# Rank-dependent slot sizes in a two-layer mixture of experts, and a tile's norm placed inside the sum of rows

## The chip, the cores and the metric

One core of a Trainium2 chip runs the whole program in one launch. The metric is the device time of one execution in microseconds. The changed kernel runs on the same core with the same inputs.

## The reference, cut to what matters

Two layers over 256 latent tokens and 256 context tokens of width 1024, all in float32. Each layer mixes tokens with four head groups, and then runs a mixture of experts with 64 routed experts, 6 per token, and one shared expert. Layer 0 routes 512 tokens (3072 assignments, 48 per expert on average), layer 1 only the 256 latent tokens (1536 assignments, 24 on average).

```python
scores = sigmoid(h @ router_w);  idx = top_k(scores + router_bias, 6)
gates = 2.5 * scores[idx] / sum(scores[idx])
y = sum over the 6 experts e of  gate * ((silu(h @ w_gate[e]) * (h @ w_up[e])) @ w_down[e])
y = y + shared expert(h);        x = x + mod[5] * y
# the next layer begins with   h = rms_norm(x) * (gain * (1 + mod[1])) + mod[0],   p = h @ w_in
```

An expert has 1024 x 768 gate and up weights and 384 x 1024 down weights: 4.72 MB, 302 MB for the 64 experts of a layer.

With the inputs that the reference draws by default, the experts sorted by how many tokens chose them have these counts. Layer 0: fullest 112, then 103, fifth 81, sixteenth 65, seventeenth 64, the twelve emptiest 24 down to 11. Layer 1: fullest 61, fifth 48, seventeenth 32, the twelve emptiest 8 down to 3.

## The kernel before, in words

**Units.** The experts are ranked by their count on the chip. A unit is one pass of 128 token slots through TensorE. The WHOLE fullest experts have a unit of 128 slots each (16 in layer 0, 4 in layer 1). The others go in pairs, 64 slots each, so that UNITS is 40 in layer 0 and 34 in layer 1. In a paired unit each contraction step is two matmuls, one on array columns 0 to 63 with one expert's weights streaming and one on columns 64 to 127 with the other's. The trace calls these 128*64, and those of a whole unit 128*128; each float32 matmul of these lines leaves two records. Assignments that don't fit their expert's slots go to an overflow list; if there are any, a loop over all 64 experts for each tile of tokens runs afterwards (more_slots). It did not run in this profile.

**Weights.** An expert's weights come as three chunks of 1.5 MB (lo, hi, down), each loaded by SP into one of 8 buffers, in the order in which the units use them (load_chunk, L847). SP waits for each load until the chunk that last held the buffer has been used: lo and hi are freed by the matmuls of L1425, down by those of L1446. `work(l)` writes the order of the units: 2 whole ones, then the pairs with the other whole ones spread among them, no whole one late. Units of the shared expert have their weights loaded once; layer 0 has four of them, two before the routed ones and two after the first and second routed one.

**A unit on the engines.** POOL gathers its 128 rows (L2475), PE transposes them (L1406), DVE copies them (L2302, L2303), PE runs gate and up (unit_up: lo, then hi, L1425), ACT and DVE make the activation (L1728, L2166), PE transposes it (L1437) and ACT copies it (L1734), PE runs down (L1446), ACT and DVE copy it out (L1747, L2321), and POOL scatters the rows to y_d (L2481). DVE makes the ranks, capacities and slot addresses while PE runs the shared expert (L2215 to L2248), PE turns them into lists (L1343).

**The sum of rows (`combined`).** After the last unit, SP loads for each tile of 128 tokens the six rows of each token (yrow, three buffers, L887), and after the third of these loads the next layer's first two modulation rows (load_mod, L757). PE sums five of the six rows with diagonal matrices (L948), DVE adds the sixth (L1837), adds PE's sum, multiplies and adds to xs (L1843 to L1845), ACT squares (L1523), DVE and ACT make the standard deviation (L1853, L1525), DVE makes h (`finished`, L1830 to L1832), PE transposes h (L962), ACT copies it. PE's order is: tile 0, tile 1, transposes of tile 0, tile 2, transposes of tile 1, tile 3, transposes of tiles 2 and 3. `finished(i - 1)` stands on DVE behind the adds of tile i, and DVE waits for the modulation rows (`mod_loaded`) behind the adds of tile 0. SP then waits until PE has summed tile 2, issues the next layer's projection weights (load_projection, L762 to L765) and its 16 small loads (load_small, L769 to L772), and all engines meet at the end of the phase. The first projection matmuls follow (L976). The row of L913 below is from the start of the program, where the modulation is computed with matmuls on four 32-column tiles.

## Time and profile before

| | |
|---|---|
| runs before | 2777.4, 2782.1, 2788.86 us; median 2782.1 |
| profiled execution | 2787.68 us, its span 2785.5 us |
| TensorE busy | 2377.6 us, 85% of the span |
| VectorE, ScalarE, GpSimd busy | 27%, 16%, 12% |
| mean granted TensorE clock | 0.941 of 2.4 GHz |
| DMA | 776.12 MB, mean 279 GB/s |
| routed units of layer 0 | from about 624 to 1467 us of the span |
| sum of rows, layer 0 to layer 1 | 1484.6 to 1564.7 us |
| routed units of layer 1 | from about 1970 to 2736 us |

Times of rows are microseconds from the start of the span. A busy TensorE is not one at its peak: its matmuls overlap, and while it waits for weights nothing is counted. What bounds a stage is read from which wait ends last there, and from the DMA share and rate of that stretch.

### The profile page before, as it was taken

The numbers are of one execution on the slowest core, as the hardware profiler recorded it, in microseconds if no ns is written. First come the engines' busy times: TensorE is split into PE (matmuls) and PEld (weight loads), VectorE is DVE, ScalarE is ACT, GpSimd is POOL, SyncE is SP. The second block draws the span as 40 slices with busy tenths as digits, with TensorE's granted clock in tenths as the row PEclk, the third lists the DMA queues.
The fourth block names the chain that finished last, engine by engine and source line by source line (L and its number), as shares of the span: only waits on it lengthen the run. The fifth ranks groups of instructions, "written<-read, shape, count | busy, mean of one in ns | idle before, by whom it ended". The sixth has DMA issues, their size and how long they took to land. (4 is left out here: it accounts for less than half of the span.)

```text
span 2785.5 us, 38829 instructions
## 1 busy us (share of the span) xinstructions
PE 2377.6 (85%) x16229; PEld 1276.6 (46%) x16229; DVE 742.8 (27%) x1589; ACT 443.1 (16%) x901; POOL 323.0 (12%) x380
## 2 busy tenths in 40 slices
PE   4998999989989998889884898998888788788885
PEld 2457744455444444444431356854443334343332
DVE  1364545353111111111102446464210101111111
ACT  1232343210000000000000132352000000000000
POOL 0005300000111111110100003400111111000000
PEclk8999999999999999999997899999999999999997
DMA  8000088445999999999985310015699999999993
GB/s 304 25 21 32 4 317 312 170 153 179 413 427 415 405 409 393 396 399 380 418 345 215 118 46 17 4 66 207 251 425 427 421 422 421 414 413 411 411 413 127
DMA packets 126595, 776.12 MB, mean 279 GB/s; under 512 B 36760, under 2 KB 45096, under 8 KB 69968
## 3 DMA queue, kind: packets, MB, share of 16 engines
q1 hardware_dynamic: 103376, 735.75, 65.4%
q0 software_dynamic: 23040, 37.82, 3.7%
q8 instruction: 133, 2.18, 0.3%
q14 instruction: 46, 0.38, 0.0%
HBM read 770.98 MB, written 44.44 MB: 293 GB/s over the span
## 5 line engine op out<-in xcount | busy, mean ns | idle before, releaser
L1425 PE MATMUL banks<-arena,htreg 128*64 128x384 f32 (+1 forms) x4288 | 922.4, 522 | 184.7 <-DMA arena<-in_exp_w_gu 177.6
L1425 PEld LDWEIGHTS banks<-arena,htreg 128*64 128x64 f32 (+1 forms) x4288 | 455.0, 156 | 622.8 <-issue 388.8
L1446 PE MATMUL banks<-arena,modreg 128*64 128x512 f32 (+1 forms) x1608 | 433.4, 599 | 23.9 <-issue 19.7
L2166 DVE TENSOR_TENSOR modreg<-modreg,banks 128x384 f32<-128x384 f32 x80 | 44.3, 554 | 1063.1 <-ACT modreg L1728 1059.4
L1446 PEld LDWEIGHTS banks<-arena,modreg 128*64 128x64 f32 (+1 forms) x1608 | 155.4, 148 | 245.5 <-issue 242.0
L2475 POOL DMA_INDIRECT htreg<-h_d,lsg x74 | 76.2, 1029 | 1059.6 <-PE banks L1406 929.7
L988 PE MATMUL banks<-arena,htreg 128*128 128x512 f32 (+3 forms) x480 | 159.7, 492 | 0.0
L2321 DVE COPY modreg<-banks 128x512 f32<-128x512 f32 x74 | 51.2, 692 | 319.7 <-PE banks L1446 319.7
L2481 POOL DMA_INDIRECT y_d<-modreg,lst x74 | 73.4, 992 | 478.3 <-DVE modreg L2321 477.7
L1728 ACT ACTIVATE modreg<-banks 128x384 f32<-128x384 f32 x80 | 39.2, 490 | 562.9 <-PE banks L1425 562.9
L1734 ACT ACTIVATE modreg<-banks 128x384 f32<-128x384 f32 x80 | 39.2, 490 | 517.9 <-PE banks L1437 517.9
L988 PEld LDWEIGHTS banks<-arena,htreg 128*128 128x128 f32 x480 | 89.9, 191 | 65.5 <-issue 61.5
L1747 ACT ACTIVATE modreg<-banks 128x512 f32<-128x512 f32 x74 | 44.2, 597 | 448.5 <-PE banks L1446 448.5
L948 PE MATMUL banks<-arena 128*128 128x512 f32 x120 | 60.5, 668 | 56.1 <-DMA arena<-y_d 56.1
L976 PE MATMUL banks<-htreg,arena 128*128 128x512 f32 x192 | 85.7, 609 | 14.4 <-SPq L667 13.7
L1406 PEld LDWEIGHTS banks<-const,htreg 128*128 128x128 f32 x592 | 73.8, 193 | 46.6 <-issue 31.6
L1406 PE MATMUL banks<-const,htreg 128*128 128x128 f32 x592 | 84.2, 286 | 9.1 <-DMA htreg<-h_d,lsg 9.1
L1290 PE MATMUL banks<-arena,htreg 128*128 128x512 f32 x192 | 83.2, 593 | 0.0
L1245 PE MATMUL banks<-arena 64*128 64x512 f32 (+3 forms) x144 | 73.0, 589 | 2.6 <-ACT arena L1662 2.6
L948 PEld LDWEIGHTS banks<-arena 128*128 128x128 f32 x120 | 25.8, 219 | 89.6 <-issue 89.6
L976 PEld LDWEIGHTS banks<-htreg,arena 128*128 128x128 f32 x192 | 37.5, 196 | 61.7 <-issue 46.6
L1080 PE MATMUL banks<-arena 64*64 64x64 f32 x1536 | 59.2, 224 | 0.9 <-issue 0.6
(393 smaller groups left out, 2183.9 us busy)
## 6 DMA issues: line engine op xcount, KB each, us to landing
arena<-in_exp_w_gu SPq DMA_DIRECT2D x256, 1536.0 KB, 23.9
arena<-in_exp_w_down SPq DMA_DIRECT2D x128, 1536.0 KB, 23.4
arena<-in_w_mod SPq DMA_DIRECT2D x32, 1024.0 KB, 10.2
arena<-y_d SPq DMA_DIRECT2D x6, 3072.0 KB, 16.8
modreg<-in_w_mod SPq DMA_DIRECT2D x14, 1024.0 KB, 8.5
modreg<-mod_d SPq DMA_DIRECT2D x20, 512.0 KB
arena<-in_w_in SPq DMA_DIRECT2D x4, 2048.0 KB, 9.4
arena<-in_w_out SPq DMA_DIRECT2D x2, 4096.0 KB, 14.1
```

Of the source, the lines that this page charges most:

```text
L948: last = mm(ps[4 + 2 * (i % 2) + half][:], diag[i % 2][:, k, :], yrow[i % YB][:, k, 512 * half:512 * half + 512], start=(k == 0), stop=(k ...
L976: last = mm(ps[ct % 2][:], win_qkv[:, k, tok(ct)], hT[:, k, :], start=(k == 0), stop=(k == KD - 1))
L988: last = mm(ps[2 + n % 4][:, lo:w], hT[:, k, tok(t)], win[g][:, k, lo:w], start=(k == 0), stop=(k == KD - 1))
L1080: last = mm(out[r, at + HALF * g:at + HALF * g + HALF], lhs(r, g), rhs(r, g), start=True, stop=True)
L1245: mm(ps[s % 2][:, 0:nk * P], q_, k_, start=True, stop=True).then_inc(scores_psum.sem, 1)
L1290: last = mm(ps[2 + n % 2][:], mixT[:, k, tok(t)], wout[:, k, 512 * half:512 * half + 512], start=(k == 0), stop=(k == KD - 1))
L1406: last = pe.transpose(ps[k // 4][:, tok(k % 4)], src[:, k, :], ident)
L1425: last = mm(gu_bank(n, half)[rows, 0:DE], src[:, k, rows], up4[q][:, i, DE * half:DE * (half + 1)], start=(k == 0), stop=(k == KD - 1))
L1446: last = mm(ps[4 + half][rows, :], actT[:, k, rows], dn3[q][:, k, 512 * half:512 * half + 512], start=(k == 0), stop=(k == KE - 1))
L2321: dve.tensor_copy(outs[r % 2][:, 512:1024], ps[5][:]).then_inc(unit_y.sem, 1)
L2475: pool.indirect_dma_start(out=slots[r % 2], out_offset=None, in_=h_d, in_offset=bass.IndirectOffsetOnAxis(ap=lsg1[:, u:u + 1], axis=0), bo ...
L2481: pool.indirect_dma_start(out=y_d, out_offset=bass.IndirectOffsetOnAxis(ap=lst1[:, u:u + 1], axis=0), in_=outs[r % 2], in_offset=None, bou ...
```

## The change

Layer 0 has 4 whole units instead of 16. In both layers the fifth to sixteenth fullest experts (BIG = 12) have 96 slots and share a unit with one of the twelve emptiest, which has 32. The others stay in pairs of 64. Layer 0 then has 34 units instead of 40, layer 1 has 34 as before. A unit of 96 and 32 slots is run as four 32-column tiles per contraction step, three with the one expert's weights and one with the other's (tiles_of). DVE's ranks, capacities and addresses follow the three sizes. In the sum of rows, DVE waits for the modulation rows and finishes tile i - 1 before its adds of tile i; SP issues the modulation rows after the second load of rows, and the small loads ahead of its wait and of the projection weights.

```diff
--- before.py
+++ after.py
@@ -38,7 +38,8 @@
 NT = 4
 MIX = 1024
 HALF = P // 2
-WHOLE = (16, 4)
+WHOLE = (4, 4)
+BIG = (12, 12)
 UNITS = tuple((NE + w) // 2 for w in WHOLE)
 CHUNK = 3072
 SLOTS = 8
@@ -339,7 +340,7 @@
         unit_hot = carve(stat, 288, NE)
         row64 = carve(stat, 352, NE)
         shift_by = carve(stat, 416, NE)
-        keycol, rankcol, dropcol = (carve(stat, 480 + i, 1) for i in range(3))
+        keycol, rankcol, dropcol, latecol = (carve(stat, 480 + i, 1) for i in range(4))
         maxcnt = sb("maxcnt", [1, 8], I32)
         RING = 4
         eid = sb("eid", [P, NE], U32)
@@ -571,7 +572,9 @@
         def work(l):
 
             whole = [(u, (u,)) for u in range(WHOLE[l])]
-            paired = [(u, (u, u + UNITS[l] - WHOLE[l])) for u in range(WHOLE[l], UNITS[l])]
+            big = range(WHOLE[l], WHOLE[l] + BIG[l])
+            paired = [(u, (u, u + NE - big.stop)) for u in big]
+            paired += [(u, (u, u + UNITS[l] - big.stop)) for u in range(big.stop, UNITS[l])]
             order = [whole.pop(0) for _ in range(FIRST)]
             early = len(paired) - 4
             for i in range(len(paired)):
@@ -886,13 +889,13 @@
                         sp.wait_ge(out_psum.sem, out_psum.at(2 * l + 1, 2 * (i - YB) + 2))
                     sp.dma_start(yrow[i % YB], y_d.rearrange("(t p k) d -> t p k d", p=P, k=CODES)[i, :, 0:TOPK, :]
                                  ).then_inc(yrow_loaded[i % YB].sem, 16)
-                    if i == YB - 1 and l + 1 < DEPTH:
+                    if i == 1 and l + 1 < DEPTH:
                         load_mod(l + 1, 0, range(2))
                 if l + 1 < DEPTH:
+                    load_small(l + 1)
                     sp.wait_ge(y_added.sem, y_added.at(l, YB))
                     sp.wait_ge(out_psum.sem, out_psum.at(2 * l + 1, 2 * YB))
                     load_projection(l + 1)
-                    load_small(l + 1)
                     phase_end(sp, "sp")
             for i in range(2):
                 sp.wait_ge(resid_ready.sem, resid_ready.at(2 * DEPTH - 1, i + 1))
@@ -1380,9 +1383,13 @@
                                       start=(k == 0), stop=(k == KE - 1))
                     last.then_inc(X["dn"].sem, 1)
 
-                def rows_of(n):
-
-                    return [slice(0, P)] if len(WORK[l][n][1]) == 1 else [slice(0, HALF), slice(HALF, P)]
+                def tiles_of(n, qs):
+
+                    if len(qs) == 1:
+                        return [(slice(0, P), qs[0])]
+                    if WORK[l][n][0] < WHOLE[l] + BIG[l]:
+                        return [(slice(32 * i, 32 * i + 32), qs[i == 3]) for i in range(4)]
+                    return [(half_rows[j], qs[j]) for j in range(2)]
 
                 def weights(n, part):
 
@@ -1421,7 +1428,7 @@
                         for i in range(4):
                             k = 4 * PARTS.index(part) + i
                             for half in range(2):
-                                for rows, q in zip(rows_of(n), qs):
+                                for rows, q in tiles_of(n, qs):
                                     last = mm(gu_bank(n, half)[rows, 0:DE], src[:, k, rows], up4[q][:, i, DE * half:DE * (half + 1)],
                                               start=(k == 0), stop=(k == KD - 1))
                         last.then_inc((lo_used if part == "lo" else gu_psum).sem, 1)
@@ -1442,7 +1449,7 @@
                     pe.wait_ge(actT_ready.sem, actT_ready.at(l, n + 1))
                     for k in range(KE):
                         for half in range(2):
-                            for rows, q in zip(rows_of(n), qs):
+                            for rows, q in tiles_of(n, qs):
                                 last = mm(ps[4 + half][rows, :], actT[:, k, rows], dn3[q][:, k, 512 * half:512 * half + 512],
                                           start=(k == 0), stop=(k == KE - 1))
                     last.then_inc(down_psum.sem, 1)
@@ -1826,6 +1833,8 @@
 
                 def finished(i):
                     u, s = 2 * (l + 1), i // 2
+                    if i == 0:
+                        dve.wait_ge(mod_loaded.sem, mod_loaded.at(u, 4))
                     dve.wait_ge(std_ready.sem, std_ready.at(u, i + 1))
                     link(dve.reciprocal(stat[:, 12 + i:13 + i], stat[:, 8 + i:9 + i]))
                     link(stt(h[:, i, :], xs[:, i, :], stat[:, 12 + i:13 + i], mod[:, 1, s, :], ALU.mult, ALU.mult))
@@ -1836,6 +1845,8 @@
                     dve.wait_ge(yrow_loaded[i % YB].sem, yrow_loaded[i % YB].at(l, i // YB + 1))
                     stt(acc[:, t, :], yrow[i % YB][:, BY_PE, :], gate[:, i, BY_PE:TOPK], acc[:, t, :], ALU.mult, ALU.add
                         ).then_inc(y_added.sem, 1)
+                    if i and l + 1 < DEPTH:
+                        finished(i - 1)
                     dve.wait_ge(y_added.sem, y_added.at(l, i + 1))
                     for half in range(2):
                         cols = slice(512 * half, 512 * half + 512)
@@ -1845,10 +1856,6 @@
                         ins = tt(xs[:, t, cols], xs[:, t, cols], acc[:, t, cols], ALU.add)
                     ins.then_inc(resid_ready.sem, 1)
                     if l + 1 < DEPTH:
-                        if i == 0:
-                            dve.wait_ge(mod_loaded.sem, mod_loaded.at(2 * (l + 1), 4))
-                        else:
-                            finished(i - 1)
                         dve.wait_ge(squares_ready.sem, squares_ready.at(2 * (l + 1), i + 1))
                         ts(stat[:, 4 + i:5 + i], stat[:, i:i + 1], 1.0 / D, EPS, ALU.mult, ALU.add).then_inc(meansq_ready.sem, 1)
                 if l + 1 < DEPTH:
@@ -2156,7 +2163,7 @@
 
                 n_t = NOUT[l]
                 nt_ = slice(0, n_t)
-                U_, W_ = UNITS[l], WHOLE[l]
+                U_, W_, G_ = UNITS[l], WHOLE[l], BIG[l]
                 lo64 = slice(0, NE)
 
                 def unit_times(n):
@@ -2214,8 +2221,9 @@
                 sorted_round(0)
                 link(ts(row64[lo64], key[lo64], keycol[lo64], None, ALU.is_gt))
                 link(red(rankcol[lo64], row64[lo64], AX, ALU.add))
-                link(ts(dropcol[lo64], rankcol[lo64], float(U_), float(U_ - W_), ALU.is_ge, ALU.mult))
-                link(tt(rankcol[lo64], rankcol[lo64], dropcol[lo64], ALU.subtract))
+                link(ts(dropcol[lo64], rankcol[lo64], float(U_), -float(U_ - W_ - G_), ALU.is_ge, ALU.mult))
+                link(ts(latecol[lo64], rankcol[lo64], float(NE - G_), -float(NE - U_), ALU.is_ge, ALU.mult))
+                link(ts(rankcol[lo64], rankcol[lo64], dropcol[lo64], latecol[lo64], ALU.add, ALU.add))
                 link(ts(unit_hot[lo64, 0:U_], K("experts")[lo64, 0:U_], rankcol[lo64], None, ALU.is_equal))
                 if n_t == 2:
                     unit_times(0)
@@ -2223,11 +2231,13 @@
                     shared_out(0)
                 dve.wait_ge(rank_psum.sem, rank_psum.at(l, 1))
                 link(dve.tensor_copy(rank, ps[0][:, 0:NE]))
-                link(ts(shift_by, rank, float(U_), float(HALF), ALU.is_ge, ALU.mult))
-                link(ts(cap, rank, float(W_), float(HALF), ALU.is_lt, ALU.mult))
-                link(ts(cap, cap, float(HALF), None, ALU.add))
-                link(tt(over[:, nt_, :], pos[:, nt_, :], bc(cap, 1, n_t), ALU.is_ge))
-                link(tt(adr[:, nt_, :], pos[:, nt_, :], bc(shift_by, 1, n_t), ALU.add))
+                link(ts(shift_by, rank, float(U_), 2.0, ALU.is_ge, ALU.mult))
+                link(stt(shift_by, rank, float(NE - G_), shift_by, ALU.is_ge, ALU.add))
+                link(ts(cap, rank, float(W_), 1.0, ALU.is_lt, ALU.add))
+                for end in (W_ + G_, NE - G_):
+                    link(stt(cap, rank, float(end), cap, ALU.is_lt, ALU.add))
+                link(stt(over[:, nt_, :], bc(cap, 1, n_t), 32.0, pos[:, nt_, :], ALU.mult, ALU.is_le))
+                link(stt(adr[:, nt_, :], bc(shift_by, 1, n_t), 32.0, pos[:, nt_, :], ALU.mult, ALU.add))
                 link(stt(adr[:, nt_, :], over[:, nt_, :], float(NT * P * 2), adr[:, nt_, :], ALU.mult, ALU.add))
                 for i in range(n_t):
                     link(tt(ohp, onehot[:, i], bc(adr[:, i, :], 1, TOPK), ALU.mult))
@@ -2265,9 +2275,11 @@
                              ALU.mult, ALU.mult))
 
                 def overflow_addresses():
-                    link(ts(base, rank, float(U_), float(HALF * U_ - U_ + W_), ALU.is_ge, ALU.mult))
+                    link(ts(base, rank, float(U_), float(HALF * U_ - U_ + W_ + G_), ALU.is_ge, ALU.mult))
                     link(tt(base, base, rank, ALU.add))
-                    link(tt(cnt, cnt, cap, ALU.subtract))
+                    link(ts(shift_by, rank, float(NE - G_), float(32 * U_ - NE + U_), ALU.is_ge, ALU.mult))
+                    link(tt(base, base, shift_by, ALU.add))
+                    link(stt(cnt, cap, -32.0, cnt, ALU.mult, ALU.add))
                     link(red(cntmax[:, 0:1], cnt, AX, ALU.max))
                     link(ts(cntmax[:, 1:2], cntmax[:, 0:1], float(P), None, ALU.add))
                     link(dve.tensor_copy(maxcnt[0:1, 0:1], cntmax[0:1, 1:2]))
```

## Rows read from the trace of the kernel before

**Rows 1.** The page: the busy line and the DMA rate of the 40 slices.
```profile
PE 2377.6 (85%) x16229; PEld 1276.6 (46%) x16229; DVE 742.8 (27%) x1589; ACT 443.1 (16%) x901; POOL 323.0 (12%) x380
...
GB/s 304 25 21 32 4 317 312 170 153 179 413 427 415 405 409 393 396 399 380 418 345 215 118 46 17 4 66 207 251 425 427 421 422 421 414 413 411 411 413 127
```

**Rows 2.** Windows: busy time per engine, PE clock, DMA share, GB/s.
```profile
700.00:750.00 50.00, 48.53 (x258) 21.89 (x259) 7.61 (x12) 4.73 (x9) 7.05 (x7) 1.00 1.00 409
750.00:800.00 50.00, 45.67 (x189) 24.74 (x188) 4.98 (x8) 3.68 (x8) 7.98 (x8) 0.97 1.01 428
...
1400.00:1450.00 50.00, 42.25 (x220) 20.33 (x218) 5.07 (x8) 3.15 (x6) 1.95 (x2) 0.93 0.96 398
...
700.00:1450.00 750.00, 669.52 (x3064) 334.24 (x3066) 92.52 (x148) 58.88 (x112) 95.36 (x95) 0.96 0.99 405
...
2010.00:2680.00 670.00, 562.27 (x2866) 264.46 (x2866) 75.81 (x120) 47.30 (x90) 71.44 (x71) 0.95 1.00 416
```

**Rows 3.** Waits from 700 to 1450: total us, times, longest.
```profile
PE banks L1425 <- DMA arena<-in_exp_w_gu: 74.3, 34, 5.2
```

**Rows 4.** Timeline of PE in layer 0: start, us, instructions, idle before.
```profile
712.01 5.38 PE L1425 MATMUL banks<-arena,htreg 128*64 128x384 f32 x32
...
729.47 5.33 PE L1425 MATMUL banks<-arena,htreg 128*64 128x384 f32 x32
...
1110.04 5.32 PE L1425 MATMUL banks<-arena,htreg 128*128 128x384 f32 x16
...
1121.68 5.37 PE L1446 MATMUL banks<-arena,modreg 128*64 128x512 f32 x24
1126.88 5.33 PE L1425 MATMUL banks<-arena,htreg 128*64 128x384 f32 x32
```

**Rows 5.** Timeline at the program's start: two steps on four 32-column tiles.
```profile
26.44 1.92 PE L913 MATMUL banks<-htreg,crep 128*32 128x512 f32 x16 [1.41 <-DMA htreg<-in_w_mod]
26.89 0.13 PEld L913 LDWEIGHTS banks<-htreg,crep 128*32 128x32 f32 x4 [0.30 <-issue]
27.32 0.13 PEld L913 LDWEIGHTS banks<-htreg,crep 128*32 128x32 f32 x4 [0.30 <-issue]
```

**Rows 6.** Timeline of layer 1's list making.
```profile
1943.31 1.11 DVE L2240 TENSOR_SCALAR arena<-const,arena 128x128 f32<-128x128 f32 x4
1945.78 3.10 PE L1343 MATMUL banks<-arena,modreg 128*64 128x128 f32 x24
```

**Rows 7.** Timeline of the sum of rows in layer 0.
```profile
1484.55 3.00 SPq L887 DMA_DIRECT2D arena<-y_d  x3
...
1487.60 2.07 SPq L757 DMA_DIRECT2D modreg<-mod_d  x4
...
1495.99 19.08 PE L948 MATMUL banks<-arena 128*128 128x512 f32 x40 [30.05 <-DMA arena<-y_d]
...
1509.20 1.06 ACT L1523 ACTIVATE hreg<-xs 128x1024 f32<-128x1024 f32 x1 [42.62 <-DVE xs L1845]
...
1516.16 0.15 DVE L1853 TENSOR_SCALAR stat<-stat 128x1 f32<-128x1 f32 x1 [7.06 <-DMA modreg<-mod_d]
...
1524.44 1.97 PE L962 MATMUL banks<-const,hreg 128*128 128x128 f32 x8 [9.37 <-DVE hreg L1832]
...
1526.20 10.68 PE L948 MATMUL banks<-arena 128*128 128x512 f32 x20
...
1536.99 0.39 SPq L762 DMA_DIRECT2D arena<-in_w_in  x1
...
1543.54 10.55 PE L948 MATMUL banks<-arena 128*128 128x512 f32 x20
...
1555.69 7.68 SPq L772 DMA_DIRECT2D convw<-in_gdn_conv_w  x6
...
1564.74 42.89 PE L976 MATMUL banks<-htreg,arena 128*128 128x512 f32 x96 [0.72 <-ACTq L667]
```

**Rows 8.** DMA issues: count, KB each, median us from issue to landing.
```profile
arena<-in_w_in SPq DMA_DIRECT2D x2, 3072.0 KB, 20.1
```

## The prediction

> **What bounds the kernel now.** I read the page first, then the windows of each stage, then the waits and timelines inside them. TensorE is busy 85% of the span, which says nothing yet. The DMA rate by slices shows two plateaus at about 380 to 430 GB/s, one for the experts of each layer, and little traffic between them [rows 1]. The 604 MB of expert weights (302 MB a layer) pass there, and the change leaves them as they are: the question is how near each plateau stands to what DMA can do.
>
> Layer 1 is at its bound: over 670 us the DMA share is 1.00 at 416 GB/s, TensorE busy 84% [rows 2]. Layer 0 runs 750 us at 405 GB/s, share 0.99 [rows 2]. Its fifteen 50 us windows fall into two kinds: seven with share 1.00 or more, which average 416 GB/s (the first, 409, and the second, 428, are two of them), and eight below, which average 395 (the last, 398, is one) [rows 2]. So layer 0 reaches the pace of layer 1 about half of the time and loses some 5% in the other half. What happens there is in PE's timeline. A pair of experts needs 17.5 us of PE (729.47 less 712.01, no wait between), a whole unit 16.8 (1126.88 less 1110.04) [rows 4]. At 416 GB/s the weights of a pair (9.44 MB) need 22.7 us, those of a whole unit 11.3. A whole unit is thus bound by PE by 5.5 us, a pair by DMA by 5.2, and 8 buffers are too few to carry the difference across each alternation. Where whole unit and pair follow each other DMA finds no free buffer; where two pairs follow PE waits: 74.3 us in 34 waits [rows 3].
>
> **Part 1: six units fewer in layer 0.** Twelve whole units become six pairs' worth: 40 routed units become 34, which takes 6 x 17.2 = 103 us of work off PE, the mean of 17.5 and 16.8. But the same 302 MB remain, so only DMA's idle part comes back. The order of layer 0 becomes that of layer 1: 30 pairs with 2 whole units among them. The stretch from 700 to 1450 moved 750 x 405 = 303.8 MB; at 416 that is 730 us, 20 us less. Bounds: if the low windows are low for a reason of DMA's own and only the missing 1% of share comes back, 7.5 us; if all goes at the best window, 428 GB/s, 710 us, 40 us less. I take 20, since layer 0's own full windows and layer 1 agree on 416. Before 700 us nothing changes: the first two whole units and the four shared ones stay where they are. Nor does the tail, the last pairs in both orders. GpSimd issues 6 gathers and 6 scatters fewer, with the same valid rows; I count it at nothing, for it waits on PE anyway.
>
> **Part 2: four 32-column tiles, in 12 units of each layer.** The stationary columns stay 128 in all and the moving columns 384 or 512; the number of matmuls doubles. Rows of 32-column tiles exist: two steps of four tiles with 512 moving columns, 16 records, took 1.92 us, with the fresh weight loads 0.43 us apart for half a step, and each four loads in 0.13 [rows 5]. That is 0.86 us per step in stream, 0.96 with the ends counted. A paired step of the same width takes 5.37/6 = 0.895 [rows 4]. So four tiles cost between 0.96 and 1.07 times the pair. At 1.07 a 96/32 unit needs 18.6 us of PE, still 4 below DMA's 22.7. Value: 0 in both layers, hidden by DMA; without that cover 12 x 1.1 = 13 us per layer at the upper end. For the range I allow 0 to 5, for buffers that come free a little later.
>
> The Trainium skill speaks against it here: "TensorE: Matmul & The Clock Gate", Part 3, section "Measured speedup vs the span model", gives three column tiles a speedup of 2.38, not 3, so 1.26 times the ideal. By it, as an estimate, the step would be 1.26 x 0.895 = 1.13 us where the row shows 0.96 at most, and the unit 21.6 us, still below 22.7, so the sum would be the same.
>
> **Part 3: DVE's addresses.** One small instruction more before the ranks and two after, on 64 columns or fewer, each below the 0.28 us of a 128-column one (1.11 for four) [rows 6]: 0.8 us at most. What hides it: in layer 1 DVE's first four slot rows are done at 1944.4 and PE takes them up at 1945.8, held by the shared expert's down [rows 6]; layer 0 has two more tiles' work but also a whole down before it. The reserve is 1.4 us, and if it were gone the price is 0.8 in each layer. The three more in the overflow addresses stand behind the lists. Taken as 0.
>
> **Part 4: the norm inside the sum of rows.** Before, DVE has tile 0's mean square to make at 1510.4, but stands in the wait for the modulation rows until 1516.16; these were issued at 1487.6 behind three loads of 3.1 MB [rows 7]. Then it sums tile 1 and finishes tile 0 without a pause, so that PE, done with tile 1 at 1515.1, gets h of tile 0 at 1524.4 [rows 7]. From there each tile costs 17.3 us (1543.54 less 1526.20) [rows 7]: PE's sum 10.6, then DVE's adds of the second half, ACT's square and root, DVE's finish, PE's transposes, all in series, and the TensorE clock falls to half in each pause.
>
> After: the rows land at about 1508, one load of 3.1 MB (7.5 us) earlier. At 1510.4 DVE makes tile 0's mean square, takes the sixth row of tile 1 (1.3 us), and finishes tile 0 (2.8) at 1514.9. PE goes on at 1515.1, just after its own tile 1. From then on DVE sets the pace: tile 1's sum with tile 0's finish took 8.2 us (1516.16 to 1524.4) [rows 7], and 1.4 to 1.6 us are spent each time until ACT has squared what DVE added. So 9.8 us per tile, while PE has 8.4 (19.08 less 10.68, twenty records at full clock) plus 1.1 to 2.0 for transposes [rows 7], about the same. DVE ends the adds of tiles 1, 2, 3 at 1519.1, 1529, 1539; root 1.7, finish 2.8, transposes 2.0 and copy 0.6 give 1546. The stage ended at 1564.7 [rows 7], so 18 us less. The projection's first weights are now issued when PE ends tile 2, at 1526 instead of 1537; such a load of 3 MB took 20 us at the median [rows 8], so it lands at 1546, just in time: I take 1 us off. SP's issues for projection and small loads ran from 1536.99 to 1563.37, 26.4 us for both [rows 7]. Starting at 1526 they would end at 1552 and hold the phase; with the 16 small ones, half of this time by an estimate from their share, moved to 1507 to 1520, before SP's wait ends and behind the fourth load of rows, SP ends at about 1539. So their move is worth part of the 17. Bounds: 9, if the two loads swapped only move the wait from the modulation rows to tile 2's rows, and 20, if PE's 8.4 + 1.1 set the pace. Value: 17 us.
>
> **The sum.** The profiled execution took 2787.7 (span 2785.5, 2.2 around it). 2787.7 - 20 - 17 = 2750.7. The profiled one stood 5.6 above the median of 2782.1, so the same 37 off the median gives 2745.
>
> **The rivals.**
> (a) Layer 0 gains nothing, since DMA was the bound anyway. For it: share 0.99. Against: 395 against 416 GB/s in half of the windows. Then part 1 gives 0 to 8: 2745 + 16 = 2761.
> (b) Slower: the four tiles don't run side by side, or three that stream the same weights get in each other's way. The place is L1425 and L1446 in 24 units. It decides from the point where such a unit's PE time passes 22.7 us, which is a step 1.33 times a pair's (the 1.7 us of transposes apart). At twice the pair's step the unit needs 33 us, 24 x 10.6 = 254 us more, less the 17 of part 4 and what part 1 can't give: about 3020. Against: the 0.96 us of a four-tile step [rows 5], though those tiles shared one set of weights.
> (c) An expert overflows its slots. The counts have 81 against 96, 64 against 64 and 24 against 32, so no; the loop would load all 64 experts four times, 1208 MB, 2900 us.
> (d) DMA was idler than its share says and the whole plateau goes to 428: 2745 - 20 = 2725.
> (e) The norm's move gives only 9: 2753. It stays in the forecast's range.
>
> **How the numbers follow.** Forecast with (e) 0.66, (a) 0.15, (d) 0.08, (b) 0.06, (c) 0.01, no change at all (both parts fall out) 0.04. The range takes the bounds of the likely case and (a) and (d): from 2725 to 2766, where 2766 is (a) with 12 us of part 4. What can be told from no change is 0.5%, 14 us: below 2768 is faster. (a) ends faster too, save for a corner of it of about 0.03. So faster 0.86, same 0.07, slower 0.07.
>
> **What would show it.** Right: in layer 0 the windows of the plateau at share 1.00 and 414 to 418 GB/s, PE's waits for expert weights above 140 us, records 128*32 with a step of 0.64 to 0.72 us for 384 columns; layer 0's last scatter about 20 us earlier; the first transposes 6 us after DVE's first mean square, not 14, tiles of L948 about 10 us apart, and L976 about 60 us after the first load of rows, not 80. Layer 1's plateau as long as before. Wrong: a rate that stays at 405 with share 1.00 (a), 128*32 steps of over 0.9 us (b), or the wait of 7 us turning up before tile 2's rows.

## The result, and the profile after

The changed kernel takes 2746.76 us (median of 4 runs, 2744.78 to 2758.16) beside 2785.48 us of the kernel before: 38.7 us less, ratio 0.9872 with a 95% interval of 0.9834 to 0.991. The prediction was 2745, 37 us less.

The profiled execution of after is the longest of the four, 2758.16 us. I split its span, and that of every kernel below, at events that all of them have: the first load of expert weights of each layer, the first load of rows (SP's first y_d load), the first projection matmul of layer 1, and the end.

| kernel | to the first expert load | experts, layer 0 | sum of rows | mix, layer 1 | experts, layer 1 | rest | span |
|---|---|---|---|---|---|---|---|
| before | 593.1 | 891.5 | 80.2 | 370.9 | 814.4 | 35.5 | 2785.5 |
| after | 605.4 | 870.4 | 60.6 | 370.7 | 812.5 | 36.9 | 2756.4 |
| norm_only | 594.1 | 890.1 | 60.9 | 367.9 | 814.2 | 35.6 | 2762.8 |
| units_only | 594.4 | 874.3 | 78.9 | 371.0 | 813.3 | 34.1 | 2766.0 |
| l1_halves | 589.8 | 870.0 | 60.9 | 370.8 | 816.2 | 34.3 | 2742.0 |
| units37 | 588.1 | 882.9 | 60.6 | 367.6 | 813.9 | 35.5 | 2748.6 |
| finish_late | 590.4 | 869.3 | 75.0 | 371.0 | 812.9 | 36.7 | 2755.2 |
| mod_late | 592.2 | 871.5 | 65.4 | 369.1 | 813.8 | 34.6 | 2746.5 |
| small_late | 596.0 | 869.9 | 67.2 | 371.2 | 813.2 | 36.2 | 2753.7 |
| before_light | 594.4 | 884.0 | 80.1 | 371.0 | 809.9 | 34.3 | 2773.7 |
| light_sorted | 589.8 | 890.8 | 79.6 | 368.2 | 805.0 | 34.9 | 2768.4 |
| after_light | 596.1 | 868.6 | 61.8 | 371.1 | 808.8 | 34.7 | 2741.1 |
| shared_late | 596.0 | 862.1 | 61.6 | 371.1 | 813.4 | 36.3 | 2740.5 |
| best | 603.7 | 855.3 | 61.3 | 371.1 | 811.9 | 35.6 | 2738.9 |

After against before: 21.1 us less with layer 0's experts, 19.6 less in the sum of rows, 2.1 less in layer 1's mix and experts, 1.4 more at the end. The first column is code that no kernel here changes; it spreads over 588 to 606 us, and after's profile has 12.3 us more of it than before's. So its span shows 29.1 us less, its runs 38.7. The other columns are the ones to compare; kernels whose layer 0 is that of after spread over 869.3 to 874.3 us in the second, so one profile's difference there is good to some 2 to 5 us.

The page of after, its busy line and the DMA rate of the slices, which answer to [rows 1]:

```profile
span 2756.4 us, 42823 instructions
...
PE 2312.5 (84%) x18275; PEld 1204.2 (44%) x18275; DVE 729.2 (26%) x1575; ACT 433.0 (16%) x883; POOL 310.9 (11%) x368
...
GB/s 307 14 32 33 3 292 330 174 120 172 357 428 422 410 415 417 418 414 414 406 389 238 112 46 17 5 74 237 260 426 426 413 414 420 419 420 416 415 413 127
```

PE lost 65 us of busy time; layer 0's plateau (the rates from 428 to 406 in the first half of the line) is now nearly as high as layer 1's. Windows inside the two plateaus of after: busy us of PE, PEld, DVE, ACT, POOL, then clock, DMA share, GB/s.

```profile
700.00:1300.00 600.00, 494.37 (x3526) 221.11 (x3527) 67.30 (x107) 41.10 (x79) 77.25 (x77) 0.93 1.00 416
2050.00:2600.00 550.00, 456.02 (x3064) 208.77 (x3058) 62.40 (x99) 38.37 (x73) 57.39 (x57) 0.94 1.00 419
```

The same windows of before:

```profile
700.00:1300.00 600.00, 538.02 (x2422) 270.19 (x2423) 74.96 (x120) 47.83 (x91) 83.29 (x83) 0.97 0.99 405
2050.00:2600.00 550.00, 455.88 (x2304) 215.73 (x2304) 60.64 (x96) 38.36 (x73) 57.34 (x57) 0.94 1.00 419
```

Layer 0 went from 405 to 416 GB/s, layer 1 stayed at 419. PE's waits of after from 700 to 1450 us, which answer to [rows 3]:

```profile
PE banks L1432 <- DMA arena<-in_exp_w_gu: 118.4, 49, 4.5
```

PE's timeline of after in layer 0 (L1432 and L1453 are L1425 and L1446 of before; before's are [rows 4]):

```profile
771.08 6.80 PE L1432 MATMUL banks<-arena,htreg 128*32 128x384 f32 x64 [2.96 <-DMA arena<-in_exp_w_gu]
...
785.94 5.37 PE L1432 MATMUL banks<-arena,htreg 128*32 128x384 f32 x64 [1.69 <-DMA arena<-in_exp_w_gu]
...
802.93 5.36 PE L1453 MATMUL banks<-arena,modreg 128*32 128x512 f32 x48
```

A gate-and-up chunk on four 32-column tiles takes 5.37 us, a pair's on two 64-column tiles 5.38 [rows 4]; a down chunk 5.36 against 5.37. Twice the instructions, the same time. The 6.80 has the slow clock's share in it: it stands behind a wait.

The sum of rows of after (SP's queue, PE, DVE, ACT), which answers to [rows 7] (L951, L1530, L1860, L965 and L979 are L948, L1523, L1853, L962 and L976 of before):

```profile
1475.73 1.46 SPq L890 DMA_DIRECT2D arena<-y_d  x2
...
1477.24 2.48 SPq L760 DMA_DIRECT2D modreg<-mod_d  x4
1479.77 17.98 SPq L890 DMA_DIRECT2D arena<-y_d  x2
...
1486.26 19.66 PE L951 MATMUL banks<-arena 128*128 128x512 f32 x40 [28.54 <-DMA arena<-y_d]
...
1501.23 0.15 DVE L1860 TENSOR_SCALAR stat<-stat 128x1 f32<-128x1 f32 x1 [1.28 <-ACT hreg L1530]
...
1501.32 5.33 SPq L772 DMA_DIRECT2D small<-in_gqa_qk_g  x1
...
1503.01 1.28 DVE L1840 SCALAR_TENSOR_TENSOR hreg<-xs,stat,modreg 128x1024 f32<-128x1024 f32 x1
...
1505.76 1.04 PE L965 MATMUL banks<-const,hreg 128*128 128x128 f32 x8
...
1506.63 8.75 PE L951 MATMUL banks<-arena 128*128 128x512 f32 x20
1506.69 3.62 SPq L772 DMA_DIRECT2D small<-in_swa_sink  x1
...
1516.78 8.75 PE L951 MATMUL banks<-arena 128*128 128x512 f32 x20
1517.01 0.47 SPq L765 DMA_DIRECT2D arena<-in_w_in  x1
...
1533.64 1.97 PE L965 MATMUL banks<-const,hreg 128*128 128x128 f32 x8 [7.24 <-DVE hreg L1841]
1536.33 44.27 PE L979 MATMUL banks<-htreg,arena 128*128 128x512 f32 x96 [0.72 <-ACTq L670]
```

DVE's mean square of tile 0 is at 1501.23 and PE has tile 0's h at 1505.76, 4.5 us later (before it was 14.0 from 1510.4, where DVE could have made it, and 8.3 from 1516.16, where it did). Tiles of L951 start 10.15 us apart (17.3 before), at full clock (8.75 us for twenty records instead of 10.6). The first projection matmul stands at 1536.33, 60.6 us after the first load of rows (80.2 before).

### The profile page after: what moved, and what is told of

Its sections match the earlier page's. It is cut to its first block and busy times, and to the rows that moved or that the text cites. A ratio compares the mean times of both kernels' runs of the same rounds, so it can differ in the third digit from the quotient of the medians.

```text
span 2756.4 us, 42823 instructions
## 1 busy us (share of the span) xinstructions
PE 2312.5 (84%) x18275; PEld 1204.2 (44%) x18275; DVE 729.2 (26%) x1575; ACT 433.0 (16%) x883; POOL 310.9 (11%) x368
## 5 line engine op out<-in xcount | busy, mean ns | idle before, releaser
L1432 PE MATMUL banks<-arena,htreg 128*32 128x384 f32 (+2 forms) x5824 | 879.5, 532 | 229.2 <-DMA arena<-in_exp_w_gu 221.5
L1432 PEld LDWEIGHTS banks<-arena,htreg 128*32 128x32 f32 (+2 forms) x5824 | 408.2, 137 | 675.0 <-issue 520.0
L1453 PE MATMUL banks<-arena,modreg 128*32 128x512 f32 (+2 forms) x2184 | 400.4, 597 | 31.8 <-issue 27.8
L1453 PEld LDWEIGHTS banks<-arena,modreg 128*32 128x32 f32 (+2 forms) x2184 | 134.4, 127 | 244.9 <-issue 240.9
L2487 POOL DMA_INDIRECT htreg<-h_d,lsg x68 | 70.0, 1029 | 1066.7 <-PE banks L1413 925.0
L1735 ACT ACTIVATE modreg<-banks 128x384 f32<-128x384 f32 x74 | 36.3, 491 | 569.1 <-PE banks L1432 569.1
L2493 POOL DMA_INDIRECT y_d<-modreg,lst x68 | 67.5, 992 | 459.7 <-DVE modreg L2333 459.1
L1741 ACT ACTIVATE modreg<-banks 128x384 f32<-128x384 f32 x74 | 36.3, 490 | 523.2 <-PE banks L1444 523.2
L951 PE MATMUL banks<-arena 128*128 128x512 f32 x120 | 57.5, 640 | 55.6 <-DMA arena<-y_d 55.6
L979 PE MATMUL banks<-htreg,arena 128*128 128x512 f32 x192 | 88.2, 623 | 14.9 <-SPq L670 14.2
L1413 PEld LDWEIGHTS banks<-const,htreg 128*128 128x128 f32 x544 | 67.1, 194 | 47.6 <-issue 35.8
L1413 PE MATMUL banks<-const,htreg 128*128 128x128 f32 x544 | 78.6, 288 | 9.1 <-DMA htreg<-h_d,lsg 9.1
L1248 PE MATMUL banks<-arena 64*128 64x512 f32 (+3 forms) x144 | 79.9, 640 | 1.4 <-ACT arena L1669 1.4
L979 PEld LDWEIGHTS banks<-htreg,arena 128*128 128x128 f32 x192 | 38.3, 201 | 63.8 <-issue 48.3
L951 PEld LDWEIGHTS banks<-arena 128*128 128x128 f32 x120 | 24.4, 207 | 87.3 <-issue 87.3
```

The lines of the kernel that those rows point to most:

```text
L951: last = mm(ps[4 + 2 * (i % 2) + half][:], diag[i % 2][:, k, :], yrow[i % YB][:, k, 512 * half:512 * half + 512], start=(k == 0), stop=(k ...
L979: last = mm(ps[ct % 2][:], win_qkv[:, k, tok(ct)], hT[:, k, :], start=(k == 0), stop=(k == KD - 1))
L1248: mm(ps[s % 2][:, 0:nk * P], q_, k_, start=True, stop=True).then_inc(scores_psum.sem, 1)
L1413: last = pe.transpose(ps[k // 4][:, tok(k % 4)], src[:, k, :], ident)
L1432: last = mm(gu_bank(n, half)[rows, 0:DE], src[:, k, rows], up4[q][:, i, DE * half:DE * (half + 1)], start=(k == 0), stop=(k == KD - 1))
L1453: last = mm(ps[4 + half][rows, :], actT[:, k, rows], dn3[q][:, k, 512 * half:512 * half + 512], start=(k == 0), stop=(k == KE - 1))
```

## The experiments

Each ratio is against the kernel before on the same chip, with its 95% interval; times of kernels that ran on different chips are compared by their ratios. The stages are one profiled execution each. "Stage 0" is the table's third column.

### The two parts alone: norm_only, units_only

norm_only is the kernel before with the edits of the sum of rows alone:

```diff
-                    if i == YB - 1 and l + 1 < DEPTH:
+                    if i == 1 and l + 1 < DEPTH:
                         load_mod(l + 1, 0, range(2))
...
+                    load_small(l + 1)
                     sp.wait_ge(y_added.sem, y_added.at(l, YB))
                     sp.wait_ge(out_psum.sem, out_psum.at(2 * l + 1, 2 * YB))
                     load_projection(l + 1)
-                    load_small(l + 1)
...
+                    if i and l + 1 < DEPTH:
+                        finished(i - 1)
                     dve.wait_ge(y_added.sem, y_added.at(l, i + 1))
...
```

units_only is the changed kernel with these undone, so that only the units and their addresses differ from before.

> The kernel before with part 4 alone: the modulation rows after the second load of rows, the small loads ahead of the wait, and DVE's finish of tile i - 1 ahead of its adds of tile i. My theory (the two parts add up): from the first load of rows to the first projection matmul 61 us instead of 80, and 17 to 20 us off the whole, ratio 0.993 to 0.994. Rival (the whole gain is in the experts' stage, and what the norm gains is lost in the wait for the projection weights): ratio 0.998 or more. Rival (layer 0's experts gained nothing and the norm gave it all): ratio 0.986.

> The changed kernel with part 4 undone: 34 units in layer 0 and four 32-column tiles for 12 units in each layer. My theory: layer 0 from the first expert load to the first load of rows takes about 870 us instead of 891, the sum of rows 80 us as before, ratio 0.992 to 0.993. Rival (DMA was the bound anyway): 885 us or more and ratio 0.997 or more.

Measured: norm_only 2762.91 us beside 2783.21, ratio 0.9928 [0.9912, 0.9944], 20.3 us less. units_only 2767.34, ratio 0.9949 [0.9932, 0.9966], 15.9 us less. The sum is 36.2; both together gave 38.7. Within their intervals the parts add up, and each moved its own column: sum of rows 60.9 against 80.2, stage 0 874.3 against 891.5.

### Does the four-tile unit cost anything: l1_halves

Layer 1 has no expert above 64 tokens, so its units can go back to pairs of 64 (from the changed kernel):

```diff
-BIG = (12, 12)
+BIG = (12, 0)
```

> The changed kernel with layer 1 back at plain pairs of 64 and 64 slots (the same 34 units, no 32-column tiles there). My theory: the four-tile step costs what a pair's step costs and DMA is the bound, so layer 1's stage stays within 2 us of 812 and the time is the changed kernel's within noise, ratio to before 0.986 to 0.988. Rival (32-column tiles cost something that DMA hides only in part): layer 1's stage 5 to 13 us shorter, ratio 0.982 to 0.985.

Measured: 2747.5 beside 2783.21, ratio 0.9871 [0.9853, 0.9889] against 0.9872 for the changed kernel. Layer 1's experts took 816.2 against 812.5 us. A pair's chunks in its timeline:

```profile
2408.04 5.37 PE L1453 MATMUL banks<-arena,modreg 128*64 128x512 f32 x24
2414.87 5.38 PE L1432 MATMUL banks<-arena,htreg 128*64 128x384 f32 x32 [1.46 <-DMA arena<-in_exp_w_gu]
```

So 12 four-tile units in layer 1 cost nothing that can be told, and gain nothing there.

### Half of the step: units37

```diff
-WHOLE = (4, 4)
-BIG = (12, 12)
+WHOLE = (10, 4)
+BIG = (6, 12)
```

> The changed kernel with 10 whole units and 6 units of 96 and 32 slots in layer 0: 37 units, between 40 and 34. My theory (a whole unit is bound by PE and 8 buffers can't carry it over to the next pair): the stage from first expert load to first load of rows lies between 870 and 891, nearer to 870, since whole units then stand apart by three pairs and more: 872 to 880. Rival (the gain goes with the number of units, 3.5 us a unit): 881. Rival (something else in the change, not the unit count, gave the 21 us, the four tiles for instance): 885 or more.

Measured: 2755.11 beside 2783.21, ratio 0.9906 [0.989, 0.9921]; stage 0 882.9. From 16 to 10 whole units it lost about 8 us, from 10 to 4 about 12. My 872 to 880 missed, by less than the 2 to 5 us that one profile's stage is good to, so the stage alone doesn't decide. The times of the runs say the same: 28.1 us less, of which norm_only has 20.3, leaves 7.8 for the units, half of units_only's 15.9. That is the rival's gain in proportion to the number of units. A loss that came only where whole units and pairs alternate densely would have gone first.

### Inside the sum of rows: finish_late, mod_late, small_late

Each is the changed kernel with one edit undone: `finished(i - 1)` and its wait behind the adds of tile i again; the modulation rows behind the third load of rows again; the small loads behind the projection weights again.

```diff
 finish_late
-                    if i and l + 1 < DEPTH:
-                        finished(i - 1)
...
                     if l + 1 < DEPTH:
+                        if i == 0:
+                            dve.wait_ge(mod_loaded.sem, mod_loaded.at(2 * (l + 1), 4))
+                        else:
+                            finished(i - 1)
 mod_late
-                    if i == 1 and l + 1 < DEPTH:
+                    if i == YB - 1 and l + 1 < DEPTH:
                         load_mod(l + 1, 0, range(2))
 small_late
-                    load_small(l + 1)
                     sp.wait_ge(y_added.sem, y_added.at(l, YB))
...
                     load_projection(l + 1)
+                    load_small(l + 1)
```

> The changed kernel with DVE's finish of tile i - 1 back behind its adds of tile i, and the wait for the modulation rows back behind tile 0's adds; the loads stay in their new order. From the first load of rows to the first projection matmul (80.2 us before, 60.6 changed). My theory (the series of adds, square, root, finish, transposes sets 17.3 us per tile, and only the finish ahead of the adds breaks it): the modulation rows no longer hold DVE, which gives some 3 to 5 us, and the tiles stay 17 us apart: 73 to 77 us. Rival (the late modulation rows were the whole loss): 61 to 64 us.

> The changed kernel with the modulation rows loaded after the third load of rows again. The same stretch. My theory: DVE's finish of tile 0 waits until about 31.5 us after the first load of rows instead of 27, and what follows shifts by that: 64 to 66 us. Rival (the wait is covered by tile 2's rows, which would now come earlier): 61 us.

> The changed kernel with the 16 small loads behind the projection weights again. The same stretch. My theory: SP's issues of both take 26 us and start when PE ends tile 2, 39.6 us after the first load of rows, so that SP holds the phase until 66 to 67 us. Rival (the phase's end is set by ACT alone): 60.6 us.

Measured: finish_late 2761.36 (before 2779.37), ratio 0.994 [0.9919, 0.9962], sum of rows 75.0; mod_late 2749.57, 0.9883 [0.9845, 0.992], 65.4; small_late 2753.14, 0.9896 [0.9854, 0.9937], 67.2. PE's timeline of finish_late:

```profile
1497.18 9.97 PE L951 MATMUL banks<-arena 128*128 128x512 f32 x20
1512.03 1.97 PE L965 MATMUL banks<-const,hreg 128*128 128x128 f32 x8 [4.89 <-DVE hreg L1839]
1513.79 10.19 PE L951 MATMUL banks<-arena 128*128 128x512 f32 x20
```

Tiles are 16.6 us apart again, with a pause of 4.9 and the slower clock behind it. DVE's timeline of mod_late, and PE's of small_late:

```profile
1494.09 0.16 DVE L1839 RECIPROCAL stat<-stat 128x1 f32<-128x1 f32 x1 [3.39 <-DMA modreg<-mod_d]
```

```profile
1524.59 1.97 PE L965 MATMUL banks<-const,hreg 128*128 128x128 f32 x8 [7.25 <-DVE hreg L1841]
1533.05 7.24 PE L979 MATMUL banks<-htreg,arena 128*128 128x512 f32 x13 [6.49 <-SPq L670]
```

The finish ahead of the adds is worth 14.4 of the 19.6 us, the modulation rows 4.8, the small loads 6.6. They overlap (25.8 in all): each undone one is the next thing that is late. These prices are by the column; the three ratios stand in the same order, though the intervals of mod_late and small_late overlap. In small_late h is done at 1526.6, and PE stands 6.5 us until SP, which still issues small loads, reaches the end of the phase.

### What bounds layer 0: before_light, light_sorted, after_light

The prediction said that a whole unit is bound by PE. These kernels leave half of the gate and up contraction of the routed experts out, so that PE has less to do per unit, with the same loads.

```diff
 before_light, after_light
-                        for i in range(4):
+                        for i in range(4 if is_shared(l, n) else 2):
...
 light_sorted, beside it: all whole units first, then all pairs
-            for i in range(len(paired)):
-                order.append(paired[i])
-                while whole and (len(order) - i - 1) * early < (i + 1) * WHOLE[l]:
-                    order.append(whole.pop(0))
-            return order + whole
+            return order + whole + paired
```

> The kernel before with half of the contraction steps of gate and up left out in every routed unit (two of four of each chunk; all weights are still loaded and waited for), so that a unit needs 11 to 12 us of PE and a whole unit no more than its weights need. My theory (whole units slow layer 0 through PE alone): layer 0's plateau rises from 405 to 415 to 420 GB/s, as in layer 1, whose own plateau stays at 416 to 420. Rival (something of DMA's own makes layer 0 slower, such as its larger scatters): it stays at 405 to 408. Rival (DMA could do 428 throughout if PE let it): both layers rise to 425 and more.

> The kernel before with half of gate and up left out in every routed unit, as in the earlier light run, and in both layers all whole units ahead of all pairs. The light run left layer 0's plateau at 409 GB/s with share 0.99, although PE had half of its work: PE's throughput is not what holds it. Theory A (where a whole unit and a pair follow each other, PE's bursts and the loads' order leave too few loads in flight; a unit's kind alone costs nothing): the light pairs' part of layer 0 runs at 417 to 419 GB/s with share 1.00, and the whole units' part at 410 and more. Theory B (each unit costs DMA something of its own, by its gather and scatter): the whole units' part, with twice as many units per byte, runs at 400 or less, the pairs' at 417. Theory C (layer 0's larger scatters cost it): 409 in both parts.

> The changed kernel with half of gate and up left out in every routed unit. Layer 0's plateau was 416 to 418 GB/s at share 1.00 with all the work. If DMA is the bound there, the plateau stays at 416 to 419 and the stage at 866 to 871 us less what the two early routed units gain (10 us), so 860 to 866; if PE still held it back, it rises to 425 and more and the stage falls below 850.

Measured: before_light 2772.23 (before 2779.37), ratio 0.9981 [0.9968, 0.9994]; light_sorted 2776.96 (before 2784.56), 0.9983 [0.9967, 1.0]; after_light 2738.36 (the same before), 0.9832 [0.98, 0.9864]. Windows of before_light, then of light_sorted (its whole units run until about 857 us), then of after_light:

```profile
700.00:1300.00 600.00, 431.52 (x1681) 201.94 (x1679) 75.58 (x121) 48.01 (x91) 83.03 (x83) 0.86 0.99 409
2050.00:2600.00 550.00, 360.23 (x1552) 159.83 (x1552) 61.15 (x97) 38.33 (x73) 58.44 (x58) 0.85 1.00 419
```

```profile
700.00:850.00 150.00, 142.81 (x479) 80.64 (x478) 29.34 (x48) 19.11 (x38) 36.08 (x36) 1.00 1.00 415
750.00:800.00 50.00, 49.44 (x164) 27.59 (x164) 10.32 (x17) 6.31 (x12) 13.00 (x13) 1.00 1.01 422
800.00:850.00 50.00, 43.37 (x143) 24.27 (x142) 8.03 (x13) 5.96 (x12) 10.99 (x11) 1.00 0.98 397
900.00:1400.00 500.00, 323.25 (x1342) 139.68 (x1340) 50.74 (x81) 31.55 (x60) 47.88 (x48) 0.82 1.00 405
```

```profile
700.00:1300.00 600.00, 394.07 (x2286) 165.43 (x2284) 63.78 (x101) 40.59 (x77) 74.25 (x75) 0.85 1.01 418
```

before_light took 106 us of busy time off PE in the first window and layer 0 still moved 409 GB/s, where 415 to 420 were expected. Stage 0 is 884.0: 7.5 us less, not the 20 that the other order gives, and most of the 7.5 are gained before the plateau (251 GB/s from 650 to 700 us where before has 206, 425 from 700 to 750 where it has 409).

light_sorted is the surprise. Its whole units ran at 425 and 422 GB/s while PE was busy throughout; from 795 us on PE waits for their weights as well, and the rate is 397. Its pairs, PE busy 65%, ran at 405 with share 1.00. There DMA is hardly ever short of work and yet slower than the pairs of layer 1 in the same execution (share 1.01, 420 GB/s from 2050 to 2600 us). None of the theories in the expectation carries that.

after_light stays at 418: with the changed units, DMA bounds layer 0 and PE's work hardly matters any more. Its stage, 868.6 against 870.4, missed the expected 860 to 866.

### Further along: shared_late, best

Until about 750 us PE, not DMA, is the bound in after; its first wait for weights in layer 0's pairs ends at 762 us. Windows of after, 50 us each:

```profile
700.00:750.00 50.00, 50.00 (x469) 20.73 (x472) 7.47 (x12) 4.32 (x9) 9.02 (x9) 1.00 0.98 391
750.00:800.00 50.00, 37.66 (x374) 15.55 (x370) 5.03 (x8) 3.15 (x6) 6.01 (x6) 0.93 1.01 427
```

From 636 to 705 us PE ran, without a wait for weights, the first two whole units and the two late units of the shared expert, and from 650 to 700 DMA moved 157 GB/s. shared_late puts these two at places 8 and 18 of the order, where PE has time to spare, and loads their weights again (9.44 MB more in all). best does the same with fewer whole units, and with pairs of 64 alone in layer 1.

```diff
 shared_late
-            order = [(None, (i,)) for i in range(EARLY)]
+            order = [(None, (i,)) for i in range(EARLY)] + routed
             for i in range(EARLY, NOUT[l]):
-                order += [routed.pop(0), (None, (i,))]
-            return order + routed
+                order.insert(8 + 10 * (i - EARLY), (None, (i,)))
+            return order
...
 best, beside it
-WHOLE = (4, 4)
-BIG = (12, 12)
+WHOLE = (2, 2)
+BIG = (14, 0)
```

> The changed kernel with the third and fourth unit of the shared expert moved from behind the first and second routed unit to places 8 and 18 of layer 0's order, among the pairs, where PE waits for weights; the shared expert's weights (4.7 MB) are loaded again for each. It takes 2 x 17.2 = 34 us of PE out of the stretch up to 700 us in which DMA runs at 170 GB/s, and adds 9.4 MB, 23 us of DMA. My theory (layer 0 is bound by DMA but for its start): 11 us less, stage 859 instead of 870, ratio to before 0.983. Rival (a unit without loads among the pairs empties the queue as a whole unit did, or the extra loads are not hidden): 870 or more, ratio 0.987 or more.

> The same, and 2 whole units, 14 units of 96 and 32 slots in layer 0 (33 units instead of 34), and 2 whole units and 31 pairs in layer 1 (33 instead of 34, no 32-column tiles). If each whole unit costs its stage 1.3 to 2.1 us, as 16, 10 and 4 whole units gave it (890, 883 and 870 us), two fewer in each layer give 3 to 4 us in layer 0 and as much in layer 1: ratio 0.980 to 0.981. Rival (4 whole units in 34 cost nothing any more): as shared_late.

Measured, beside 2784.56 of before: shared_late 2736.68, ratio 0.9826 [0.9806, 0.9846], stage 0 862.1 (expected 859); best 2734.2 (6 runs), ratio 0.9818 [0.9796, 0.984], stage 0 855.3. Windows of shared_late, then of best:

```profile
650.00:700.00 50.00, 50.00 (x414) 22.40 (x416) 7.48 (x12) 4.73 (x9) 7.75 (x8) 1.00 0.92 344
700.00:750.00 50.00, 43.34 (x372) 18.97 (x365) 4.98 (x8) 3.65 (x7) 4.26 (x5) 0.93 1.02 426
```

```profile
700.00:1300.00 600.00, 489.45 (x3552) 218.68 (x3550) 65.14 (x104) 40.53 (x77) 70.20 (x70) 0.93 1.00 419
```

The hole in front of the plateau is mostly closed. best has the lowest time of all, by the ratios 15 us below the changed kernel; its interval overlaps that of shared_late, so the units' part of it rests on the profiles alone: 6.8 us of stage 0, where 3 to 4 were expected, and 1.5 us of layer 1's experts (813.4 to 811.9), where as much again was.

## Why the prediction came out

**The sum.** 20 + 17 = 37 us were predicted, 38.7 measured. By itself part 1 gave 15.9 us in the runs and 17 to 21 in stage 0, part 4 20.3 in the runs and 19.6 in its column. Of the rivals none came: (a) would have left stage 0 at 883 to 891, (b) needed a step of 1.33 times a pair's and the step is 1.00, the overflow loop of (c) did not run, (d) wanted 428 GB/s over the plateau, which stood at 416, and (e) 9 us where 20 came.

**Part 1: the size right, its mechanism not.** That layer 0 would take on layer 1's rate, 416 GB/s, and gain 20 us, came true. Its last scatter stands at 1459.24 where before had 1467.47, and its first expert load 12.3 us later: 20.5 us gained from load to scatter. But the step "a whole unit is thus bound by PE by 5.5 us, a pair by DMA by 5.2, and 8 buffers are too few to carry the difference across each alternation" fails. before_light takes PE's excess away and the plateau stays at 409 GB/s; light_sorted runs the whole units in one block and shows the loss in the pairs behind them, where DMA hardly waits for anybody; and units37 loses in proportion to the number of units rather than to the mix. What went with it is the low windows' reading: a share below 1.00 stood beside a low rate in before, but the rate was also low where the share was 1.00. The step was mis-sized too: 416 GB/s has the tokens' rows in it. Weights alone moved at 382 GB/s in after (229.21 MB of SP's queue from 700 to 1300 us), so a pair's need 24.7 us and a whole unit's 12.4, and PE's excess in a whole unit is 4.5. The 20 us hang on none of this: they came from one plateau set beside another. Layer 0 took on that rate for a reason that the prediction did not have, and to that extent the size was luck.

**What lowers layer 0's rate stays open, but the traces narrow it down.** Most of the loss is in single packets of the weights. These are 12 KB each; the rows' packets of 4 KB took 160 ns in before and in after. From 700 to 1300 us of before 93% of the weight packets took 460 ns and the rest longer, 478 ns in the mean; in after 96% took 460, and the mean is 469. light_sorted's pairs (930 to 1385 us) have 7.1% long ones and a mean of 480.

Two candidates lie at hand. One is the pairing: expert u runs with u + 24 in before and light_sorted, with u + 48 or u + 18 in after, so that the two streams of loads come from other places of HBM. The other is the order in which the loads take the eight buffers.

The pairing finds no support. The same pairs had a mean of 473 ns in before and 480 in light_sorted, and chunk by chunk the two are not alike (correlation -0.1 over 106 chunks, where before and norm_only, whose layer 0 is the same, have 0.67).

The order of the buffers does. By the rule in the kernel (`ring`), the pairs of light_sorted take them in the cycle 0 6 1 7 3 4 2 5, and so does the last stretch of after, from 1280 to 1385 us, with other partners and with all of PE's work. There after falls back to 407 GB/s, with 7.0% long packets and a mean of 477 ns; from 770 to 1090 us, in another cycle, it has 418 GB/s, 2.4% and 466 ns. In the six other kernels with after's order the last stretch is slower as well (means of 471 to 480 against 466 to 470). best takes a third cycle there and has no such fall. Windows of after, then of best:

```profile
1300.00:1350.00 50.00, 41.20 (x206) 19.00 (x204) 5.04 (x8) 3.16 (x6) 3.50 (x4) 0.90 1.00 406
```

```profile
1300.00:1350.00 50.00, 40.17 (x198) 18.56 (x198) 5.07 (x8) 3.16 (x6) 4.05 (x4) 0.90 1.01 422
```

The long packets come in bursts. In light_sorted's pairs a packet takes 90 and 74 ns over 460 in the first and second microsecond after GpSimd issues a unit's gather, 20 in the mean and 4 or less in the five before. SP issues loads at about the same time, so the trace doesn't say whether the gather has a part in it.

before changes its cycle several times and has its lowest stretch, 386 GB/s from 1225 to 1280 us, in one that after never takes. So the gain of part 1 goes along with the order of the buffers. That this order makes packets long, and by what, is argued and not shown: no kernel changed the buffers alone.

**PE's waits** for expert weights came to 118.4 us, not above 140. Of the 103 us of work that were to go, PE's busy time shows 65 over the span, and 53 from 700 to 1450 (669.5 [rows 2] to 616.1), with the clock down from 0.96 to 0.93, so each step after a wait runs longer (6.80 instead of 5.37 us above).

**Part 2** is confirmed exactly: step 0.671 us for 384 columns (5.37/8), 0.64 to 0.72 predicted, 1.00 times the pair's 0.673. The Trainium skill's rule ("TensorE: Matmul & The Clock Gate", Part 3, section "Measured speedup vs the span model"), from which I had estimated 1.26 times, does not carry over to this trace: the page measured three tiles, and these four float32 tiles of 32 columns with two different streams take no longer than two of 64 columns.

**Part 3** shows nowhere: layer 1's mix and experts took 2.1 us less, not more.

**Part 4** gave 19.6 to 20.3 us for 17, at the upper bound that I had put at "PE's 8.4 + 1.1". The prediction's own times end at 1546, 18.7 us before 1564.7; 1.7 of the 2.6 us that were missed are what it rounded off and took off for the projection weights, which did not come last. First transposes 4.5 us after the mean square (6 predicted), tiles 10.15 us apart (10), L979 60.6 us after the first load (60). The step that was mis-sized is SP's queue. I had the small loads out between 1507 and 1520, 13 us after the fourth load of rows. They went out at 1497.79 to 1516.9, 19 us, since two of them were held up for 5.33 and 3.62 us where the others of that kind took about 0.42. So the projection weights left at 1517.01, not when PE had ended tile 2 at 1515.4. It cost nothing here: h of tile 3 was the last thing to come.

## What to carry to other kernels

Read the bound of a stage from its plateau beside the plateau of another stage of the same program that moves the same bytes. Here the size of the gain that this gave came out and the story of who waits for whom did not; such a story takes an experiment of its own (lighten one engine, sort the order). And a share of 1.00 says that DMA is busy, not how fast it goes: look at how long its packets take. When an engine serves two chains, put the work that the other engine waits for ahead of the work that only its own queue wants: one moved call was worth 14 us. And once a plateau is at its ceiling, look at the hole in front of it: two units moved to where TensorE had time to spare paid for 9.44 MB loaded again and gave 8 us more.

## What was unexpected of the hardware

- Four 32-column tiles with two sets of weights take the time of two 64-column ones: 5.37 against 5.38 us for a gate-and-up chunk, 5.36 against 5.37 for down.
- A plateau with DMA share 1.00 is not one rate: 405 GB/s in the pairs of light_sorted's layer 0 and 420 in those of layer 1, in one execution, with the same sizes of loads, and 407 and 418 in two stretches of after's layer 0. The Trainium skill ("DMA: Bandwidth & Descriptors", section "Where 436 GB/s comes from") has the HBM side, about 358 GB/s, bind a load from HBM; here one core alone held 416 to 419 over 550 us and more, so nearer to the 435 that it gives for the fabric.
- The granted TensorE clock fell from 0.93 to 0.85 in after_light's layer 0 and DMA's rate did not move (416 and 418 GB/s).
- Issuing one small load took 5.33 us on SP, and the next one 3.62, behind the four row loads of 3.1 MB each, against 0.42 us for the ones before them. The same two were held in norm_only (5.26 and 3.62). In small_late, where they stand behind the projection weights, they took 0.44 and 0.43. That the row loads in flight held them is what this suggests; no run here separates it from other causes.
